# Query and key sums of squares in two reduced-precision passes, one chunk later, with a low part made on GpSimd

## The reference, cut to what matters

```python
def rmsnorm(x, g):
    xf = x.astype(F32)
    xf = xf * lax.rsqrt(jnp.mean(xf * xf, axis=-1, keepdims=True) + EPS)
    return xf.astype(x.dtype) * g

def rope(x, pos):
    ...
    x1, x2 = xf[..., :half], xf[..., half:]
    return jnp.concatenate([x1 * cos - x2 * sin, x2 * cos + x1 * sin], axis=-1).astype(x.dtype)

    qa = rope(rmsnorm(qa.reshape(b, t, A_HEADS, 2, A_DH), p['q_norm_g']), pos)
    ka = rope(rmsnorm(ka.reshape(b, t, A_HEADS, 2, A_DH), p['k_norm_g']), pos)
    ...
    ob, s_new = recur(qh, kh, gh, vh)
```

## Time and profile before

| | |
|---|---|
| median of 3 runs | 2249.35 us (2248.5 to 2251.11) |
| the profiled execution's own time | 2248.97 us |
| its span, first to last instruction | 2247.2 us |
| granted TensorE clock, mean | 0.998 |
| busy, share of the span | PE 99%, PEld 94%, DVE 68%, ACT 52%, POOL 42% |
| the recurrence phase of the third head | from 405.98 us, eight chunks |

### The profile page before, as it was taken

One profiled execution on the slowest core, in us unless ns is written; L12 is line 12 of the kernel. 1 busy time (PEld: TensorE's weight loads), 2 busy tenths in 40 slices (PEclk: granted clock), 3 DMA queues, 4 the chain that ended last, 5 costly groups with the idle time before them and its releaser, 6 DMA issues. The chain is left out here.

```text
span 2247.2 us, 47821 instructions
## 1 busy us (share of the span) xinstructions
PE 2219.7 (99%) x18881; PEld 2103.6 (94%) x18881; DVE 1535.8 (68%) x2531; ACT 1158.0 (52%) x2407; POOL 938.8 (42%) x1144
## 2 busy tenths in 40 slices
PE   7999999999999999999999999999999999999999
PEld 5899998989899999989988999999999999999999
DVE  4668677776767677776676515417988888976545
ACT  6666665766666566665454512114566666643110
POOL 1145262634445362635422224442165665635431
PEclk9999999999999999999999999999999999999999
DMA  8212122131213121132689623112345555485212
GB/s 309 85 55 90 48 80 75 58 105 55 100 48 106 40 77 66 59 105 87 240 315 363 263 41 123 48 48 81 123 181 185 188 189 187 172 316 192 86 47 95
DMA packets 103514, 288.35 MB, mean 128 GB/s; under 512 B 18426, under 2 KB 26490, under 8 KB 103290
## 3 DMA queue, kind: packets, MB, share of 16 engines
q1 hardware_dynamic: 102138, 281.09, 35.6%
q10 hardware_dynamic: 1152, 4.19, 0.5%
HBM read 213.18 MB, written 63.77 MB: 123 GB/s over the span
## 5 line engine op out<-in xcount | busy, mean ns | idle before, releaser
L172 PE MATMUL ps<-xn_hi,h_w_hi 128*128 128x344 f32 x1680 | 560.5, 334 | 1.9 <-PEq L205 0.9
L172 PE MATMUL ps<-xn_hi,h_w_lo 128*128 128x344 f32 x1680 | 536.6, 319 | 0.0
L172 PE MATMUL ps<-xn_lo,h_w_hi 128*128 128x344 f32 x1680 | 536.2, 319 | 0.0
L172 PEld LDWEIGHTS ps<-xn_hi,h_w_hi 128*128 128x128 f32 x1680 | 317.0, 189 | 38.8 <-issue 25.5
L172 PEld LDWEIGHTS ps<-xn_lo,h_w_hi 128*128 128x128 f32 x1680 | 315.7, 188 | 4.8
L172 PEld LDWEIGHTS ps<-xn_hi,h_w_lo 128*128 128x128 f32 x1680 | 315.6, 188 | 0.0
L1225 POOL TENSOR_TENSOR h_w_lo<-h_w_raw,h_w_hi 128x1024 fp32r<-128x1024 f32 x58 | 149.3, 2574 | 385.3 <-ACT h_w_hi L800 349.6
L3155 DVE SCALAR_TENSOR_TENSOR x<-ps,keep_mod,x 128x344 f32<-128x344 f32 x168 | 94.2, 570 | 161.6 <-PE ps L2992 98.8
L2992 PE MATMUL ps<-f_act_lo,f_d_hi 128*128 128x344 f32 x528 | 169.4, 321 | 0.0
L2992 PE MATMUL ps<-f_act_hi,f_d_lo 128*128 128x344 f32 x528 | 168.8, 320 | 0.0
L2992 PE MATMUL ps<-f_act_hi,f_d_hi 128*128 128x344 f32 x528 | 168.4, 319 | 0.1
(11 more groups left out here) (453 smaller groups left out, 6507.0 us busy)
## 6 DMA issues: line engine op xcount, KB each, us to landing
h_w_raw<-in_w_in SPq DMA_DIRECT2D x72, 512.0 KB, 3.7
y_rows<-f_y SPq DMA_DIRECT2D x44, 516.0 KB, 2.8
f_y_pair<-y_rows SPq DMA_DIRECT2D x22, 1032.0 KB, 5.3
h_d_ada_w<-in_w_ada SPq DMA_DIRECT2D x32, 512.0 KB, 4.4
g_vp<-in_cache_v SPq DMA_DIRECT2D x32, 512.0 KB, 5.9
f_a<-in_w_ffn SPq DMA_DIRECT2D x57, 256.0 KB, 2.7
g_kp<-in_cache_k SPq DMA_DIRECT2D x28, 512.0 KB, 7.2
h_w_raw<-in_w_mix SPq DMA_DIRECT2D x24, 512.0 KB, 3.5
```

Of the source, the lines that this page charges most:

```text
L172: ins = eng.matmul(out, w[:, k * P:(k + 1) * P], x[:, k, columns], start=(k == 0 and n == 0), stop=(k == n_k - 1 and n == 2))
```

## The change

The sum over `blk` becomes two `fp32r` matmuls that accumulate in one bank: one over a high part of the squares (`sq_hi`, a ScalarE copy in `fp32r`), one over the low part (`sq_lo`, GpSimd's subtraction). The block matrix gets an `fp32r` copy once, at the stage's start. Sum, reciprocal root and the last rotary product of piece u move from chunk u to chunk u + 1. Cosine product, sine product and their sum stay in chunk u. `rg` gets a third buffer, `rt` keeps two, so the swap of piece u (u of 2 and more) now waits for `qk_ready` of piece u - 2.

```diff
+        sq_hi = [parts(f"sq_high{i}", [P, TH], F32R) for i in range(2)]
+        sq_lo = [parts(f"sq_low{i}", [P, TH], F32R) for i in range(2)]
...
+        rg.append(parts("rg2", [P, TH]))
...
@@ turn_piece, SyncE
-                turn(u, rg[u % 2][:, :], rt[u % 2][:, :], piece_read.at(h, 12 + u + 1))
+                if u >= 2:
+                    sp.wait_ge(qk_ready.sem, qk_ready.at(h, u - 1))
+                turn(u, rg[u % 3][:, :], rt[u % 2][:, :], piece_read.at(h, 12 + u + 1))
@@ ScalarE, reading piece u
-                    act.wait_ge(qk_ready.sem, qk_ready.at(h, u - 1))
-                    qk_piece(gq if kind == "q" else gk, bank, sq[u % 2][:, :], rg[u % 2][:, :])
+                    act.wait_ge(qk_ready.sem, qk_ready.at(h, max(u - 2, 0)))
+                    if u >= 2:
+                        act.wait_ge(sq_low.sem, sq_low.at(h, u - 1))
+                    qk_piece(gq if kind == "q" else gk, bank, sq[u % 2][:, :], rg[u % 3][:, :])
@@ ScalarE, chunk k
-                        qk_norm(qk_summed.at(h, k + 1), X[:, k % 2, 0:TH])
+                        act.wait_ge(qk_squared.sem, qk_squared.at(h, k + 1))
+                        act.activation(sq_hi[k % 2][:, :], sq[k % 2][:, :], ACT.Copy).then_inc(sq_high.sem, 1)
+                    if 0 < k <= 6 and not no_next(h):
+                        qk_norm(qk_summed.at(h, k), X[:, (k - 1) % 2, 0:TH])
@@ TensorE
-                pe.matmul(X[:, u, 0:TH], blk[:, :], sq[u][:, :], start=True, stop=True).then_inc(qk_summed.sem, 1)
+                pe.matmul(X[:, u, 0:TH], blk_r[:, :], sq_hi[u][:, :], start=True, stop=False)
+                pe.matmul(X[:, u, 0:TH], blk_r[:, :], sq_lo[u][:, :], start=False, stop=True).then_inc(qk_summed.sem, 1)
...
-                    if k < 6 and not no_next(h):
-                        pe.wait_ge(qk_squared.sem, qk_squared.at(h, k + 1))
-                        if k >= 2:
-                            pe.wait_ge(qk_ready.sem, qk_ready.at(h, k - 1))
-                        qk_sums(k % 2)
+                    if 0 < k <= 6 and not no_next(h):
+                        pe.wait_ge(sq_high.sem, sq_high.at(h, k))
+                        pe.wait_ge(sq_low.sem, sq_low.at(h, k))
+                        if k >= 3:
+                            pe.wait_ge(qk_ready.sem, qk_ready.at(h, k - 2))
+                        qk_sums((k - 1) % 2)
@@ GpSimd, chunk k, behind the differences
+                        pool.wait_ge(sq_high.sem, sq_high.at(h, k + 1))
+                        pool.tensor_tensor(sq_lo[k % 2][:, :], sq[k % 2][:, :], sq_hi[k % 2][:, :].bitcast(F32), ALU.subtract).then_inc(sq_low.sem, 1)
                         pool.wait_ge(piece_read.sem, piece_read.at(h, 12 + k + 1))
                         pool.wait_ge(qk_turned[k].sem, qk_turned[k].at(h, 4))
-                        pool.tensor_tensor(rg[k % 2][:, :], rg[k % 2][:, :], cos[:, cols(k % NP)], ALU.mult).then_inc(qk_cos.sem, 1)
+                        pool.tensor_tensor(rg[k % 3][:, :], rg[k % 3][:, :], cos[:, cols(k % NP)], ALU.mult).then_inc(qk_cos.sem, 1)
@@ GpSimd, chunk 6
-                            pool.wait_ge(qk_ready.sem, qk_ready.at(h, 6))
+                            pool.wait_ge(qk_ready.sem, qk_ready.at(h, 5))
@@ VectorE, chunk k
-                        rope(j, rg[u % 2][:, :], rt[u % 2][:, :])
+                        rope(j, rg[u % 3][:, :], rt[u % 2][:, :])
+                    if 0 < k <= 6 and not no_next(h):
+                        u = k - 1
                         dve.wait_ge(qk_rstd.sem, qk_rstd.at(h, u + 1))
...
-                        rope_end(j, X[:, u % 2, 0:TH], rg[u % 2][:, :], qT if u < 3 else kT)
+                        rope_end(u % NP, X[:, u % 2, 0:TH], rg[u % 3][:, :], qT if u < 3 else kT)
```

More of the change, by code:

```diff
@@ L562, in heads_stage @@
         rows = Memory(nc, "h_rows", mem.off)("rows", [H * NS, 2, P])
-        sq = [mem(f"sq{i}", [P, TH]) for i in range(2)]
+        sq = [mem("sq0", [P, TH])]
+        parts = Memory(nc, "h_parts", R3, R3 + 2 * ROW)
+        sq_hi = [parts(f"sq_high{i}", [P, TH], F32R) for i in range(2)]
+        sq_lo = [parts(f"sq_low{i}", [P, TH], F32R) for i in range(2)]
+        sq.append(parts("sq1", [P, TH]))
+        rg.append(parts("rg2", [P, TH]))
         oraw = mem("oraw", [P, T])
@@ L571, in heads_stage @@
         far = mem("far_mask", [P, P], U32)
+        blk_r = mem("blk_r", [P, P], F32R)
         spot = Memory(nc, "h_spot", early["lmask_at"], early["lmask_at"] + LEVELS * HALF * 4)
@@ L614, in heads_stage @@
         qk_squared = S("qk_squared", 6, pre=6)
+        sq_high, sq_low = S("sq_high", 6), S("sq_low", 6)
         qk_summed = S("qk_summed", 6, pre=6)
@@ L1057, in _ @@
             late_value(2)
-            pe.wait_ge(ones_ready.sem, 1)
+            pe.wait_ge(ones_ready.sem, 2)
             def piece(h, n, between=None):
@@ L1331, in _ @@
             copy(dve, c["ones_r"][:, :], c["ones128"][:, :]).then_inc(ones_ready.sem, 1)
+            copy(dve, blk_r[:, :], blk[:, :]).then_inc(ones_ready.sem, 1)
             for sig in (lv_k, st_ready, sig_used, o_normed):
```

## The result

The changed kernel takes 2266.73 us (median of 6 runs, 2264.14 to 2269.1), the kernel before in the same session 2248.93 (6 runs, 2247.2 to 2251.11). The ratio is 1.0079, with a 95% interval of 1.0068 to 1.0090: 18 us slower. The forecast was 2274 with a range of 2254 to 2281. The profiled execution of after took 2267.26 us, its span is 2265.5.

What follows compares the result with a forecast made beforehand. TensorE, busy 99%, bounds the kernel before; after the change a ring of 6.86 us per chunk outlasts TensorE's 5.93. Seven heads each 3.66 us later: 2248.97 + 7 x 3.66 = 2274.6, given as 2274, range 2254 to 2281.

Steps and rivals of the forecast that it cites:

- a ring that a buffer closes: Sine product, sum, last product, swap, cosine product, once per chunk: 6.86 us average, 3.66 us later per head; chance 0.70.
- 28 times about 1 us: Sign of being right: GpSimd waits this often and long for the swaps of pieces 2 to 5.
- The chain into it: GpSimd's subtraction, 0.92 us, goes ahead of the cosine product; chunk 1's sine product comes at 420.33, 1.57 us late.
- The saving on TensorE: Two fp32r passes replace each fp32 sum: 0.27 us saved per sum, 11.3 us for 42, if TensorE never waits.
- the swap's issue time: SyncE issues a swap's four transfers in 2.87 us on average, 2.41 at the quickest, 3.64 at the slowest.
- 6.40 at best: One turn of the ring with the quickest swap, in us; chunk 7 then 1.82 us later per head, total 2261.7.
- late landings: Each swap transfer was taken to land 1.9 us after its issue; nothing was added for later ones.
- The cover of the squares: GpSimd's squares in chunk 6 end at 454.4, TensorE reads them at 456.2: 1.8 us of cover.
- GpSimd's chain alone: Rival: swap hidden, only GpSimd's longer chain counts, 6.31 us per chunk, 10.2 us slower, total 2259; chance 0.13.
- The saving kept: Rival: the added waits end before TensorE asks, so its 11.3 us saving stays, total 2237.7; chance 0.10.

Runs made afterwards that it cites:

- e1: Changed kernel with a third buffer for the swapped copy, so the swap no longer waits for a last rotary product; 2254.85 us, ratio 1.0028.
- e5: Changed kernel with each swap cut into five transfers of the same bytes instead of four; 2282.41 us, ratio 1.0148.
- e8: e2 with GpSimd's squares in chunk 6 additionally waiting for the state update of chunk 5; 2250.73 us, ratio 1.0007.
- e2: Changed kernel with VectorE's last product of piece u-1 ahead of the rotary instructions of piece u; 2273.24 us, ratio 1.0103.
- e10: e8 without GpSimd's subtraction, TensorE's second pass reading the high part again (sums wrong in value); 2240.69 us, ratio 0.9966.
- e3: Changed kernel without GpSimd's subtraction, TensorE's second pass reading the high part again (sums wrong in value); 2256.62 us, ratio 1.0035.
- e4: Changed kernel with GpSimd's subtraction behind its cosine product instead of ahead of it; 2289.01 us, ratio 1.0181.
- e12: e11 with the high and the low part of piece 0 made ahead of chunk 0; 2242.51 us, ratio 0.9976.
- e11: e8 with the low parts made by VectorE, in its gap ahead of the rotary, instead of by GpSimd; 2246.06 us, ratio 0.9989.

## Why the prediction was right, and where it was off

**The direction and its reason.** Slower, by a ring that a buffer closes: right. In after GpSimd waited for a swap 25 times, 16.6 us in all, where the prediction has 28 times about 1 us; the sine products stand on one period; e1 (no ring) took 12 us off and e5 (ring lengthened) added 16; e8 (ring opened by the order) took off 16, its shorter path included. e2 alone of these went the other way, by the collision in chunk 6.

**The chain into it.** By the cosine product's end, predicted at 414.07, the first sine product is 414.10 - 405.98 = 8.12 us behind chunk 0; it was at 419.11 - 411.03 = 8.08. The second: predicted 420.33 - 405.98 = 14.35, measured 425.20 - 411.03 = 14.17. The subtraction took 0.91 to 0.93 in 35 of 42 cases, as predicted, and 1.17 in chunk 0 of each head. GpSimd in the third head of after, chunk 0, answers to the earlier trace rows:

```profile
417.02 1.17 POOL L1312 TENSOR_TENSOR h_parts_sq_low<-h_d_sq,h_parts_sq_high 128x344 fp32r<-128x344 f32 x1 [0.18 <-POOL h_b_level_diff L1273]
418.16 0.92 POOL L1315 TENSOR_TENSOR h_d_rg<-h_d_rg,h_cos 128x344 f32<-128x344 f32 x1
```

**The saving on TensorE.** From the transpose ahead of the sum to the second product of the piece behind it, before and after (the second product of before is in the earlier trace rows, at 413.75):

```profile
412.85 0.33 PE L1186 MATMUL ps<-keep_ident,h_b_LK 128*128 128x128 f32 x1
```

```profile
425.31 0.33 PE L1201 MATMUL ps<-keep_ident,h_b_LK 128*128 128x128 f32 x1
...
425.95 0.32 PE L172 MATMUL ps<-xn_lo,h_w_hi 128*128 128x344 f32 x1
```

That is 0.90 and 0.64: 0.26 saved per sum, where 0.27 was predicted. Chunks 3 and 5 of e8 and e10 take 5.92 to 5.97, but for one of 6.08, against the 5.93 predicted. Right, and as predicted it was not to be had in after.

**The mis-sized term: the swap's issue time.** The prediction took 2.87 us, the mean of 28 swaps of before, and from it a ring of 6.86. All 28 ring swaps of after took 2.41 to 2.63, 27 of them under 2.44, and the ring 6.45, the "6.40 at best" of the prediction. So an undisturbed head lost not 3.66 but 1.84 us (45.50 on the mean of five, against 43.66), where the prediction has 1.82 for the quickest swap; seven times, 12.9. That the two agree to 0.02 is luck in part: four turns of 6.45 instead of 6.40 are 0.2 more, and the second sine product, from which they count, came 0.18 earlier than predicted.

The mean of before did not carry over, because the change moved the swap in time. In before each of these swaps is issued 0.03 us behind ScalarE's last reading of its piece, in after 2.2 to 4.9 us behind it. Long issue times go with the early release: swaps of 2.8 us or more among the 28 are 16 in before, 15 in e1 and in e10, and 17 in e8, where the swap is released at the end of the piece or soon behind it, but none in after, 1 in e3 and 1 in e4, where the ring releases it. In after itself the swaps of pieces 0 and 1, which do not wait for the ring, took up to 3.38. What stretches a swap there I did not isolate. Of all 42 swaps of before, 21 took 2.8 us or more, and each of them has a packet of an instruction queue in its window; but so have 10 of the other 21. That is only a correlation.

**A term put at nothing: late landings.** The prediction takes 1.9 us from issue to landing for every swap, though its rows have one of 3.4. Two of the seven heads of after were not at 45.5 but at 46.82 and 48.08. In each, one swap landed late; GpSimd in the worse one:

```profile
566.26 0.94 POOL L1315 TENSOR_TENSOR h_d_rg<-h_d_rg,h_cos 128x344 f32<-128x344 f32 x1 [2.59 <-DMA h_d_rt<-h_d_rg]
```

That swap was issued in 2.41 us as all the others, and GpSimd waited 2.59 us for it. Nothing of this is caught up in these two heads, since the ring has no slack. Why a swap lands late is open. The two add 1.3 and 2.6 us to the 12.9: 16.8, as measured. With the 1.5 outside the heads that is the whole difference. The prediction's sum was 7 x 3.66 = 25.6; that 18 lies between this and the 12.7 of the quickest swaps comes from the late landings and the 1.5, and not from issue times, so the place within the range is luck.

**The cover of the squares.** Predicted to end 1.8 us ahead of TensorE's need; the prediction's own terms, 449.4 + 4.8, give 454.2 and not the 454.4 that it has, and so 2.0. GpSimd and TensorE, third head of after, against the earlier trace rows:

```profile
453.00 1.04 POOL L1279 TENSOR_TENSOR h_d_rstd_o<-h_d_oraw 128x512 f32<-128x512 f32 x1 [1.82 <-DVE h_kT L1363]
...
456.50 1.29 POOL L1282 TENSOR_TENSOR h_rstd_osq_low<-h_d_rstd_o,h_vtok_osq_high 128x512 fp32r<-128x512 f32 x1
```

```profile
459.63 0.40 PE L1120 MATMUL ps<-h_rstd_osq_low,keep_ones_r 128*128 128x512 f32 x1
```

They end at 457.79, TensorE reads at 459.63: 1.84. Right to 0.2 us.

**The rivals.** GpSimd's chain alone (predicted 2259) is e1, which measured 2254.85: 4 us less, since its four turns took 5.98, 6.29, 6.23 and 6.31 instead of 6.31 each. The saving kept (2238) came nearest in e10 (2240.69), with the ring open and no subtraction, and in e12 (2242.51), with the ring open and the subtraction on VectorE.

## What to carry to other kernels

Before moving one step of a software pipeline, list each buffer's cycle (last reader, transfer, next writer, next reader) and add it up: here a cycle of 6.45 us set the pace of a TensorE that needed 5.93 to 6.14, with GpSimd busy 43% of the span and VectorE 68%, and it had no slack for a late landing. A duration read from the trace belongs to the moment at which the instruction ran; if the change moves its release, carry the shortest and the longest and not the mean. And when an order is mended, follow every semaphore that the moved instruction raises: e2 lost 22 us to one release that had come earlier.

## What the runs showed of the hardware that I had not expected

- A VectorE product with two SBUF operands (0.52 us) beside a running GpSimd one took 1.21 (e4), 1.23 (e11), 1.34 and 1.48 (e2). Each time it ended 0.37 to 0.39 us behind the GpSimd instruction. I had seen this as 0.2 us on GpSimd's side only. What it costs here depends on which instruction releases which.
- Behind TensorE's two waits in e2 (1.11 us each in the third head, one closely behind the other) the granted clock of 458 to 464 us was 0.72, and the 81.4 us attention part took 82.96. So it was in five of the seven heads; the first and the fourth had waits of 1.26 and 1.1 at the same places and stayed at 1.00. In e4 the clock fell behind single waits of 2.13 and 2.63 us, and not behind one of 1.91. The waits at the chunk starts of after (up to 1.11 us) and of e5 (two of 1.11 and one of about 0.87 in most heads, some 7 us apart) left it at 1.00. What decides between them is open.
- The issue of a swap took from 2.41 to as much as 3.85 us (before) when it was released at the end of a piece, and at most 2.63 when released 2.2 us or more later (after). The cause is open.
